# Reordering the waits between attention, page scores and the triangular inverse in a two-layer decoder step

## What is computed

```python
def fox_sample(q, k, v, logf, k_past, v_past, logf_past):      # 8 samples, 8 heads x 64, 1024 past keys each
    c_past = jnp.cumsum(logf_past, axis=1)
    c_new = c_past[:, -1:] + jnp.cumsum(logf, axis=1)
    s_past = einsum('nqhd,nkhd->nhqk', q, k_past) * scale + cq[..., :, None] - c_past
    s_new = einsum('nqhd,nkhd->nhqk', q, k) * scale + cq[..., :, None] - cq[:, :, None, :]   # causal
    p = jax.nn.softmax(jnp.concatenate([s_past, s_new], axis=-1), axis=-1)
    return p[..., :P] @ v_past + p[..., P:] @ v

def gated_delta_chunked(q, k, v, g, beta, s0):                 # 4 heads x 128
    gc = jnp.cumsum(gch, axis=-1)
    decay = jnp.exp(jnp.where(incl, gc[..., :, None] - gc[..., None, :], -jnp.inf))
    a_mat = jnp.where(strict, einsum('...id,...jd->...ij', kb, kc) * decay, 0.0)
    t_mat = triangular_solve(a_mat, eye, left_side=True, lower=True, unit_diagonal=True)
    ...
```

## Time and profile before

| | us |
|---|---|
| median of 3 runs | 1093.09 |
| lowest and highest | 1088.87, 1093.34 |
| profiled execution | 1091.27 |
| its span, first to last instruction | 1089.6 |
| TensorE busy in the span | 971.3 (89%) |
| DVE busy | 430.4 (39%) |
| ACT busy | 237.3 (22%) |
| POOL busy | 89.0 (8%) |
| mean granted clock of TensorE | 0.962 of 2.4 GHz |

### The profile page before, as it was taken

How to read it: one execution, slowest core, us unless ns; L and a number is a source line. 1 busy time by engine, 2 the same in 40 slices (tenths; PEclk the granted TensorE clock), 3 DMA queues, 4 the chain that set the end, 5 groups by cost and what they waited for, 6 DMA issues and landing times.

```text
span 1089.6 us, 17694 instructions
## 1 busy us (share of the span) xinstructions
PE 971.3 (89%) x6606; PEld 573.9 (53%) x6606; DVE 430.4 (39%) x1116; ACT 237.3 (22%) x504; POOL 89.0 (8%) x199
## 2 busy tenths in 40 slices
PE   8999988899889999887888899999999998777685
PEld 6777766575886365443444344444454655334341
DVE  3724444454865345333333400252002463224343
ACT  3321135452401042111110221241001411010112
POOL 6333241040000000000000000000000000000000
PEclk9999998999999999999998999999999999899899
DMA  9851175794801497999999974423434799999994
GB/s 286 244 177 24 51 263 193 252 319 179 305 1 49 155 394 311 421 420 421 420 421 419 359 256 155 155 107 128 162 116 174 328 400 420 421 421 421 418 414 160
DMA packets 90060, 292.58 MB, mean 269 GB/s; under 512 B 16099, under 2 KB 52507, under 8 KB 62030
## 3 DMA queue, kind: packets, MB, share of 16 engines
q1 hardware_dynamic: 75508, 267.63, 64.0%
q0 software_dynamic: 5152, 17.05, 4.8%
q10 hardware_dynamic: 9306, 6.67, 2.0%
HBM read 286.17 MB, written 5.16 MB: 267 GB/s over the span
## 4 chain that ended last, share of the span: by engine, by line
PE 69%; DMA 20%; DVE 5%; ACT 2%; issue 2%; SPq 1%; ACTq 0%; DVEq 0%
DMA arena<-in_moe_w_up 20%; PE ps L1309 12%; PE ps L1529 10%; PE ps L865 10%; PE ps L1619 4%; PE ps L977 3%; PE ps L1295 2%; PE ps L789 2%; PE ps L990 2%; PE ps L1066 2%; PE ps L780 1%; PE ps L809 1%; PE ps L1522 1%; PE ps L1145 1%; PE ps L1135 1%
## 5 line engine op out<-in xcount | busy, mean ns | idle before, releaser
L1309 PE MATMUL ps<-arena,hT 128*32 128x512 f32 x1024 | 133.4, 672 | 52.1 <-DMA arena<-in_moe_w_up 52.1
L1529 PE MATMUL ps<-arena,hT 128*128 128x512 f32 x256 | 112.4, 599 | 0.0
L865 PE MATMUL ps<-hT,arena 128*128 128x288 f32 x448 | 110.0, 407 | 0.0
L1309 PEld LDWEIGHTS ps<-arena,hT 128*32 128x32 f32 x1024 | 37.4, 122 | 133.8 <-issue 132.3
L1295 PE MATMUL ps<-lvl,htok 128*128 128x128 f32 (+1 forms) x768 | 95.5, 281 | 7.8 <-DVE x L2488 7.7
L1295 PEld LDWEIGHTS ps<-lvl,htok 128*128 128x128 f32 x768 | 90.2, 191 | 20.9 <-issue 11.4
L865 PEld LDWEIGHTS ps<-hT,arena 128*128 128x128 f32 x448 | 84.6, 190 | 23.5 <-issue 0.5
L1529 PEld LDWEIGHTS ps<-arena,hT 128*128 128x128 f32 x256 | 48.9, 192 | 60.6 <-issue 60.2
L1393 PE MATMUL ps<-arena 128*128 128x512 f32 x112 | 55.3, 618 | 4.4 <-DVE x L2482 4.4
L1341 PE MATMUL ps<-arena 128*32 128x512 f32 x448 | 51.0, 595 | 0.0
L2474 DVE TENSOR_SCALAR hT<-ps,nw 128x128 f32<-128x128 f32 (+1 forms) x64 | 22.5, 354 | 70.3 <-PE ps L1295 70.3
(11 more groups left out here) (473 smaller groups left out, 1259.0 us busy)
## 6 DMA issues: line engine op xcount, KB each, us to landing
arena<-in_moe_w_gate SPq DMA_DIRECT2D x64, 1024.0 KB, 20.2
arena<-in_moe_w_up SPq DMA_DIRECT2D x64, 1024.0 KB, 21.7
arena<-in_moe_w_down SPq DMA_DIRECT2D x56, 1024.0 KB, 21.7
arena<-in_cache_k SPq DMA_DIRECT2D x64, 256.0 KB, 3.9
arena<-in_cache_v POOLq DMA_DIRECT2D x64, 256.0 KB, 3.8
arena<-in_w_in_odd SPq DMA_DIRECT2D x16, 1024.0 KB, 10.7
arena<-in_w_in_even SPq DMA_DIRECT2D x14, 1024.0 KB, 9.4
arena<-in_moe_w_down SPq DMA_DIRECT2D x16, 512.0 KB, 15.2
```

The source lines that it names most:

```text
L865: last = mm(ps[:, c % 4, 0:T], w[:, k, P * (c % 2):P * (c % 2 + 1)], hT[:, k, :], start=k == 0, stop=k == KD - 1)
L1309: last = mm(ps[EC * j:EC * (j + 1), q % 2, :], xgT[q % 2][:, k, EC * j:EC * (j + 1)], ring[:, sl:sl + 2, DE * k:DE * (k + 1)], start=k == ...
L1529: last = mm(ps[:, bank, :], hT[:, k, P * i:P * (i + 1)], ring[:, oslot(2 * n):oslot(2 * n) + 2, QC * k:QC * (k + 1)], start=k == 0, stop=k ...
```

## The change

- `past_sums(1)` goes from the step of head 5 to the last one (h = 8), ahead of the last head's transposes; ACT copies its result after the copy of head 7's transposed weights. TensorE waits for that copy (`ks_done` 3) before key subtile 4, and the banks of the subtiles are taken in another order (3, 4, 5, 7, 6).
- `k_scores_own` is issued before the group's last `k_scores`, in both groups.
- In group 0's softmax, subtiles 32 to 34 are turned one after the other and copied by DVE, 35 after eight of the nine turned weights; ACT has no key copy there.
- In group 1's softmax all three first `delta_rows` are issued before the turned weights, and the decay sums of the tiles stand between them: tile 0 after four turned weights, tile 1 after eight, tile 2 and the columns after the ninth.
- `delta_rows` 3, 4, 5 and the eight small output copies of group 1 are made by ACT instead of DVE.
- DVE makes level 0's mask of a tile right after that tile's key products; TensorE begins level 0 as each tile's mask is there, and waits for `sa_o` and `dl_tok` only after its first products.

```diff
+        def kt_bank(n):
+            order = (3, 4, 5, 7, 6)
+            return order[n % 5] if n < 32 else (3, 4, 7, 3)[n - 32] if n < 36 else order[(n - 36) % 5]
+        def kt_before(n):
+            return n - 5 if n < 32 or n >= 41 else (-1, -1, -1, 32, 35, 33, -1, -1, -1)[n - 32]
+        def kt_by_act(n):
+            return n % 2 == 0 and not 32 <= n < 36
-            return (3, 4, 4, 3, 4, 3)[j]
+            return (3, 4, 7, 4, 3, 4)[j]
...
+                if h == HA:
+                    past_sums(1)
                 if 1 <= h <= HA:
                     pa_transposes(h - 1)
                 if h >= 2:
                     pa_out(h - 2)
-                if h in (4, 5):
-                    past_sums(h - 4)
+                if h == 4:
+                    past_sums(0)
...
             def delta_rows(j):
-                if j == 3:
+                if j >= 3:
+                    pe.wait_ge(s.dl_tok, (2, 3, 4)[j - 3])
+                if j == 4:
                     pe.wait_ge(s.dl_cols, 1)
-                elif j >= 2:
-                    pe.wait_ge(s.dl_tok, (2, 2, 3, 4)[j - 2])
...
                     if n == 4:
                         past_bias(0)
+                        pe.wait_ge(s.ks_done, 3)
...
-                k_scores(8 * grp + 7)
                 k_scores_own(grp)
+                k_scores(8 * grp + 7, s.sa_s_ps)
                 if grp == 0:
-                    k_transpose(32)
-                    k_transpose(33)
-                    pe.wait_ge(s.kt_act, 16)
-                    pe.wait_ge(s.kt_dve, 16)
-                    weights_turned(0, range(9))
-                    k_transpose(34)
+                    for n in (32, 33, 34):
+                        k_transpose(n)
+                    weights_turned(0, range(8))
                     k_transpose(35)
+                    pe.wait_ge(s.kt_dve, kt_count(34))
+                    weights_turned(0, (8,))
...
                 else:
-                    delta_rows(0)
-                    delta_rows(1)
-                    pe.wait_ge(s.kt_act, 32)
-                    pe.wait_ge(s.kt_dve, 32)
-                    weights_turned(1, range(9))
-                    decay_sums()
-                    delta_rows(2)
+                    for j in range(3):
+                        delta_rows(j)
+                    weights_turned(1, range(4))
+                    decay_sums(0)
+                    weights_turned(1, range(4, 8))
+                    decay_sums(1)
+                    pe.wait_ge(s.dl_tok, 3)
+                    weights_turned(1, (8,))
+                    decay_sums(2)
+                    decay_columns()
...
-            pe.wait_ge(s.sa_o, 6)
-            pe.wait_ge(s.dl_tok, 6)
-            pe.wait_ge(s.dl_kk, 6)
             for l in range(7):
                 for i in inv_tiles(l):
+                    if l == 0:
+                        pe.wait_ge(s.dl_kk, 2 if i < 2 else 6)
...
+                if l == 0:
+                    pe.wait_ge(s.sa_o, 6)
+                    pe.wait_ge(s.dl_tok, 6)
...
-                if h in (5, 6):
-                    grp = h - 5
+                if h in (5, HA - 1):
+                    grp = h // (HA - 1)
...
-                if grp == 0:
-                    k_tile(32)
                 act.wait_ge(s.sa_pt_ps, grp + 1)
...
-                if grp == 0:
-                    k_tile(34)
...
+            def rows_copied(j):
+                i, m = j // 2, TOK[j // 2][1]
+                act.wait_ge(s.dl_tok_ps, j + 1)
+                A_((ktok if j % 2 == 0 else vtok)[0:m, i, :], ps[0:m, row_bank_of(j), :], ACT.Copy).then_inc(s.dl_tok, 1)
+
+            rows_copied(3)
+            act.wait_ge(s.sa_o_ps, 4)
...
+                    last = A_(dst[:, c], src[:, :, 8 * c + 4 * e:8 * c + 4 * e + 4], ACT.Copy)
+                last.then_inc(s.sa_o, 1)
+            rows_copied(4)
+            rows_copied(5)
...
-                if grp == 0:
-                    k_tile(33)
-                else:
-                    delta_rows(0)
-                    delta_rows(1)
+                for j in range(3):
+                    if grp == 0:
+                        k_tile(32 + j)
+                    else:
+                        delta_rows(j)
...
-            delta_rows(4)
-            key_products(1)
-            delta_rows(5)
-            key_products(2)
...
-            inv_m(0)
+            for i in range(3):
+                key_products(i)
+                dve.wait_ge(s.dl_kk, 2 * i + 2)
+                inv_m(0, (i,))
```

More of the change, by code:

```diff
@@ L412, in kk_ps, with kt_count @@
             return ps[0:m, b, o:o + HB * m].rearrange("p (h c) -> p h c", h=HB)
+        def kt_bank(n):
[5 more added lines that the diff above has]
+            return n % 2 == 0 and not 32 <= n < 36
+        def kt_count(n):
+            return sum(kt_by_act(a) == kt_by_act(n) for a in range(n + 1))
         def decay_cols(i, w):
@@ L974, in k_transpose @@
                 if kt_before(n) >= 0:
-                    pe.wait_ge((s.kt_act, s.kt_dve)[kt_before(n) % 2], kt_before(n) // 2 + 1)
+                    pe.wait_ge(s.kt_act if kt_by_act(kt_before(n)) else s.kt_dve, kt_count(kt_before(n)))
                 for c in range(NPAIR):
@@ L982, in page_cols, with k_scores @@
                 return ps[:, pg // 4, :].rearrange("p (j g a) -> p g j a", g=4, j=4)[:, pg % 4]
-            def k_scores(t):
+            def k_scores(t, done=None):
                 grp, pg = t // NPAGE, t % NPAGE
-                pe.wait_ge(s.kt_act, 2 * t + 2)
-                pe.wait_ge(s.kt_dve, 2 * t + 2)
+                pe.wait_ge(s.kt_act, kt_count(4 * t + 2 if t != 8 else 30))
+                pe.wait_ge(s.kt_dve, kt_count(4 * t + 3))
                 for c in range(NPAIR):
@@ L992, in k_scores @@
                                   start=False, stop=False, skip_group_check=True)
-                last.then_inc(s.kpage_free, 1)
+                last.then_inc(s.kpage_free if done is None else done, 1)
             def past_bias(grp):
@@ L1018, in delta_rows, with decay_sums, decay_columns @@
                 last.then_inc(s.dl_tok_ps, 1)
[L1020 to L1028, removed]
+            def decay_sums(i):
+                m = TOK[i][1]
+                tri = ut if i < 2 else utS
+                for h in range(HB):
+                    last = mm(ps[:, i, P * h:P * h + m], bc(gg[0:m, i, h:h + 1], [m, P]), tri,
+                              start=True, stop=True)
+                last.then_inc(s.dl_R_ps, 1)
+            def decay_columns():
                 for i in range(3):
@@ L1046, in k_scores_own @@
                         last = mm(ps[32 * bl:32 * bl + 32, 2, 0:TS], qz[:, NPAIR * (4 * grp + bl) + c, :],
-                                  qkT[:, 4 + c, TP:T], start=False, stop=(bl == 3 and c == 3), skip_group_check=True)
-                last.then_inc(s.sa_s_ps, 1)
+                                  qkT[:, 4 + c, TP:T], start=False, stop=False, skip_group_check=True)
+                last.then_inc(s.kpage_free, 1)
             def weights_turned(grp, js):
@@ L1821, in _ @@
                 A_(dDT[0:m, i, :, 0:m], dDT[0:m, i, :, 0:m], ACT.Exp).then_inc(s.dl_dtx, 1)
+            def rows_copied(j):
[4 more added lines that the diff above has]
+            act.wait_ge(s.sa_o_ps, 4)
+            for e in range(2):
+                dst = mixT[64 * e:64 * e + 64, 0:NPAIR, TP + 16:TP + 32].rearrange("p c (b q) -> p c b q", b=4)
+                for c in range(NPAIR):
+                    src = ps[64 * e:64 * e + 64, 5, P * c:P * (c + 1)].rearrange("p (b j) -> p b j", b=4)
+                    last = A_(dst[:, c], src[:, :, 8 * c + 4 * e:8 * c + 4 * e + 4], ACT.Copy)
+                last.then_inc(s.sa_o, 1)
+            rows_copied(4)
+            rows_copied(5)
+            act.wait_ge(s.dl_tok, 6)
             act.wait_ge(s.dl_scaled, 1)
@@ L2231, in _ @@
                 if grp:
-                    delta_rows(3)
-                    key_products(0)
-                dve.wait_ge(s.sa_o_ps, 2 * grp + 2)
+                    continue
+                dve.wait_ge(s.sa_o_ps, 2)
                 for e in range(2):
-                    dst = mixT[64 * e:64 * e + 64, 0:NPAIR, TP + 16 * grp:TP + 16 * grp + 16]\
-                        .rearrange("p c (b q) -> p c b q", b=4)
+                    dst = mixT[64 * e:64 * e + 64, 0:NPAIR, TP:TP + 16].rearrange("p c (b q) -> p c b q", b=4)
                     for c in range(NPAIR):
@@ L2242, in _, with inv_m @@
                     last.then_inc(s.sa_o, 1)
-            delta_rows(4)
-            key_products(1)
-            delta_rows(5)
-            key_products(2)
+            def inv_m(l, tiles):
+                for i in tiles:
+                    m = TOK[i][1]
+                    V.tensor_tensor(dMT[0:m, i, :, 0:m], dLT[0:m, i, :, 0:m],
+                                    bc(lvl[0:m, l, 0:m].rearrange("p (o c) -> p o c", o=1), [m, HB, m]),
+                                    ALU.mult).then_inc(s.dl_mt, 1)
+            for i in range(3):
```

(12 more changed lines are left out.)

4 lines of the change are left out of this document (removed).

## The result

| | before | after |
|---|---|---|
| median of 4 runs each, us | 1091.41 | 1075.36 |
| lowest and highest | 1088.87, 1093.34 | 1071.55, 1077.95 |
| ratio, 95% interval | | 0.985 (0.983 to 0.988) |
| profiled execution, its span | 1091.27, 1089.6 | 1076.39, 1074.8 |
| TensorE busy in the span | 971.3 | 964.1 |

What follows compares the result with a forecast made beforehand. It took TensorE (69% of the chain) and DMA (20%) as the bound, with TensorE's own waits counting in the changed part; 2.9 + 3.4 - 0.7 + 1.2 + 1.7 + 1.7 = 10.2 off 1091.3 gave 1081.1 us, range 1077 to 1087.

Steps and rivals of the forecast that it cites:

- gains pass through: A gain at 157 to 278 us moves all that follows by the same amount, neither shrunk nor enlarged.
- the drain: End of the prompt's attention: 2.9 us from moving page sums and bias copies, 3.4 us from full clock.
- Rival (a): Clock falls in the drain all the same, 3.4 gone and 0.7 with it: 1083.8 us; chance 0.18.
- Rival (e): Page sums or bias copies don't leave the path in the heads' steps: 1085 to 1087 us; chance 0.08.
- own-key scores: Run inside the wait for DVE's key copy, so the maximum starts 0.83 us earlier in each group.
- group 0's softmax: Weights copies end earlier without ScalarE's key tile, values start at 209.2: 1.2 us, own scores' 0.83 included.
- the inverse: Its start: copies go from DVE to ScalarE, masks run earlier, the three U end 1.7 us sooner.
- I leave this at nothing: Start of group 0's values: 0.9 us more if the clock holds, counted as nothing.
- -0.7: Loss behind group 1's bias matmuls, where the clock may fall: half between bounds 0 and 1.4 us.
- Rival (b): Clock also holds in one or both values stages and after the bias: 1078.6 us; chance 0.11.
- rival (c): Key pages of group 1: an early value load could delay a page, 2 to 4 us: 1084 to 1087; chance 0.07.
- Rival (d): Waits filled with small pieces let the clock fall for long in key pages or inverse: 1102 us; chance 0.03.

Runs made afterwards that it cites:

- drain_spin: Kernel before with six dummy 128x256 products in TensorE's wait ahead of the last head's transposes, nothing moved: 1085.25 us, ratio 0.994.
- drain_only: Kernel before with only the drain's part of the change (group 1's page sums, their copies, the wait, bank order): 1081.99 us, ratio 0.992.
- drain_undone: Changed kernel with group 1's page sums and bias copies back in the steps of heads 5 and 6: 1083.23 us, ratio 0.991 to the kernel before.
- own_undone: Changed kernel with own-key scores behind the last page's scores again, both groups: 1078.44 us, ratio 0.988 to the kernel before.
- soft_spin: Kernel before with four dummy products in each softmax wait, ahead of the turned weights, nothing moved: 1085.57 us, ratio 0.995.

## Why the prediction was right and wrong

**Right: what bounds the part, and that gains pass through.** 14.3 us gained ahead of the expert loads, 14.9 at the end.

**Right: the drain.** Order 3.1 (forecast 2.9) and clock 3.5 (3.4): the clock alone is shown by drain_spin, the two together by drain_only, and both are lost in drain_undone. The price from rows at both clocks held to 0.1 us. Rival (a) is out: the low clock did not come back in the drain in any of the eleven traces with the page sums there. Rival (e) is out with it.

**Size off: own-key scores and group 0's softmax.** The scores gave 0.65 us in place of 0.83, by own_undone in both groups. At equal clock group 0's softmax became 0.34 us shorter (7.66 to 7.32), not 1.2: my base of 8.32 held a low stretch of its own, which I had not priced, and took its end for the new order's gain. As the scores alone gave 0.65, moving the key transposes and copies cost 0.3. From the maximum to the values it was 6.18 us (6.1 forecast), in group 1 7.64 (8.0 forecast); the margin of the copies there was 0.8 us, and held. In all, the order at equal clock gave 3.12 + 0.34 + 1.82 + 2.01 = 7.3 us against 7.5: misses that cancel, which is luck.

**Size off: the inverse.** 2.0 against 1.7. ScalarE's small copies cost 0.81 us for eight, where the sum took 3 us and called them hidden. The Trainium skill ("Perfetto Trace Analysis", Optimizing Scalar/DVE Operations) led to an estimate nearer 1 us, and the trace bears that out.

**Wrong: the clock behind the drain.** The step that failed is the one that took the clock of the values and of all later stages as nothing ("I leave this at nothing"), with "-0.7" for a loss behind the bias. Order and drain's clock alone gave 7.3 + 3.5 = 10.8 us between the two profiles, where the sum without its -0.7 has 10.9. In place of the -0.7 the other low stretches gave 0.66 + 0.82 - 1.62 + 1.62 = 1.5 us at places where they come and go with the order unchanged, which is luck, and 1.7 in the values of group 1; 0.9 has no one place. The loss behind the bias is no debt of the change: that stage took 22.0 us in ten of the sixteen traces and 23.6 or more in six, 2 of 5 with the old drain and 4 of 11 with the new. Rival (b) had the right kind of miss at 0.11, but priced group 1's values at 0.9, though the earlier trace rows show 3.5 us of them at 0.51; they measured 1.7. Its counter-argument, "the matmuls ahead of them are the same", is true of the last 2.2 us, and still these values kept full clock in 7 of 9 traces against 0 of 6; why stays open.

**Open: what the medians add.** 7.3 + 3.5 + 1.7 = 12.5 us have a place. The ratios of the changed kernel's two lots stand for 16.3 (13.5 to 19.1) and 14.2 us (10.8 to 17.5), so some 2 to 4 us have none. Drain_only and drain_spin also gain more by their ratios than their drains show, but within their intervals, and soft_spin gained 5.0 with its target stage unchanged; so which of the stretches that come and go give them isn't shown. The lower end of the range, (b) with a us of spread below, was too near for that: two medians of the changed kernel lay 2.3 us apart, single executions 6.7.

**Right: no loss to DMA.** Key pages of group 1 changed by -0.02 us, so rival (c) is out. Rival (d) as well: filling waits with small pieces did not lower the clock for long; between 135 and 395 us the low clock went from 27 to 10 us.

## What to carry over

Price every low-clock stretch of the part under change from rows at both levels, also those that the change doesn't touch by its words. Count as a gain one whose long pause the new order fills, as in the drain; of the others say that they come and go, and widen the range by them: a median of few runs moves with them. Where waits ahead of dense work can't be filled with work, a few wide products that nobody reads hold the clock: 3.5 us in the drain from six of them in drain_spin. Independent small work is best put one piece at a time between the steps of a chain of waits, not behind it (1.6 us in group 1's softmax).

## What was not expected of the hardware

The granted clock fell to 1.2 GHz not only behind pauses, as the 2.87 us in the drain or 1.41 us ahead of group 0's values (in three of nine traces). It also fell behind the bias products (32 rows), with TensorE busy for the 4 us ahead of it (173.0 to 176.8 at 0.62), and in the values of group 1, behind sums 32 and columns 4 wide, again without a pause. The same kernel had low stretches at 174, 215 and 358 us in one execution, at 173, 203, 313 and 360 in the next, and at 246, 311 and 359 in the third, 10.2 to 13.7 us in all, and its single executions lay between 1071.55 and 1078.26 us. Of drain_undone they lay between 1078.4 and 1089.8. What decides in which of its places the clock falls in a given execution stays open.
